# RWKV-7 recurrence: the last product of the triangular inverse in three 64x64 corners and two PSUM banks

## What is computed

```
def step(S, inp):                       # S: (value, key) state of each head
    rt, wt, kt, vt, at, bt = inp
    S = (S * wt[:, :, None, :] + jnp.einsum('bhvk,bhk->bhv', S, at)[..., None] * bt[:, :, None, :]
         + vt[..., None] * kt[:, :, None, :])
    return S, jnp.einsum('bhvk,bhk->bhv', S, rt)
S, ys = lax.scan(step, s0, xs)
```

## Time and profile before

| | |
|---|---|
| time, median of 3 runs | 3230.78 us (3226.53 to 3233.24) |
| the profiled execution | 3236.48 us, its span 3234.70 us |
| granted clock of PE, mean over the span | 0.969 |
| PE busy | 3023.7 us (93%), 32300 matmuls and as many weight loads |
| DVE / ACT / POOL busy | 1567.6 (48%) / 955.6 (30%) / 1332.6 us (41%) |
| the 16 items of the recurrence | about 1885 to 2350 us of the span |

### The profile page before, as it was taken

How to read it: one execution, slowest core, us unless ns; L and a number is a source line. 1 busy time by engine, 2 the same in 40 slices (tenths; PEclk the granted TensorE clock), 3 DMA queues, 4 the chain that set the end, 5 groups by cost and what they waited for, 6 DMA issues and landing times.

```text
span 3234.7 us, 73556 instructions
## 1 busy us (share of the span) xinstructions
PE 3023.7 (93%) x32300; PEld 2845.5 (88%) x32300; DVE 1567.6 (48%) x2107; ACT 955.6 (30%) x1640; POOL 1332.6 (41%) x1016
## 2 busy tenths in 40 slices
PE   7999988989999999989999889999878999999997
PEld 6989856889999999978999877777777999999996
DVE  5032254237666641244322156688624866663125
ACT  4132264233111121123311246666623211111112
POOL 3322310235777743341433323333232677774320
PEclk9999998999999999999999889999989999999998
DMA  3344453322223233112422313222142122324311
GB/s 101 119 135 111 144 169 110 97 79 79 79 79 112 79 131 143 52 45 103 170 92 92 100 46 98 65 61 72 47 169 91 60 79 80 114 81 134 139 42 61
DMA packets 342471, 312.25 MB, mean 97 GB/s; under 512 B 35335, under 2 KB 303059, under 8 KB 341020
## 3 DMA queue, kind: packets, MB, share of 16 engines
q1 hardware_dynamic: 325706, 275.99, 28.3%
q10 hardware_dynamic: 16466, 31.83, 2.6%
HBM read 212.79 MB, written 94.62 MB: 95 GB/s over the span
## 4 chain that ended last, share of the span: by engine, by line
PE 43%; DVE 4%; issue 3%; ACT 1%; SPq 1%; DMA 1%; POOL 1%; ACTq 0%; DVEq 0%; POOLq 0%
PE PS L521 17%; PE PS L688 12%; PE PS L2799 2%; PE PS L2811 1%; PE PS L2805 1%; PE PS L2793 1%; DVE act_lo L2516 1%; PE PS L2919 1%; PE PS L2789 1%; PE PS L702 1%; PE PS L2785 1%; PE PS L2844 0%; SPq L496 0%; PE PS L2950 0%; PE PS L2980 0%
## 5 line engine op out<-in xcount | busy, mean ns | idle before, releaser
L521 PE MATMUL PS<-act_hi,w_hi 128*128 128x344 f32 x1992 | 641.0, 322 | 38.3 <-DVE act_lo L2150 21.2
L521 PE MATMUL PS<-act_lo,w_hi 128*128 128x344 f32 x1992 | 637.8, 320 | 0.0
L521 PE MATMUL PS<-act_hi,w_lo 128*128 128x344 f32 x1992 | 637.3, 320 | 0.0
L502 POOL CAST w_hi<-w_raw 128x1024 fp32r<-128x1024 f32 (+1 forms) x119 | 129.1, 1085 | 1078.4 <-PE PS L521 561.2
L521 PEld LDWEIGHTS PS<-act_hi,w_hi 128*128 128x128 f32 x1992 | 376.4, 189 | 43.4 <-issue 28.3
L521 PEld LDWEIGHTS PS<-act_hi,w_lo 128*128 128x128 f32 x1992 | 376.4, 189 | 0.0
L521 PEld LDWEIGHTS PS<-act_lo,w_hi 128*128 128x128 f32 x1992 | 376.4, 189 | 0.0
L688 PE MATMUL PS<-T,wq_S 128*128 128x258 f32 x2880 | 365.7, 283 | 0.0
L688 PE MATMUL PS<-act_hi,wq_A 128*128 128x258 f32 x1920 | 364.5, 282 | 0.0
L688 PEld LDWEIGHTS PS<-T,wq_S 128*128 128x128 f32 x2880 | 354.4, 189 | 0.0
L688 PEld LDWEIGHTS PS<-act_hi,wq_A 128*128 128x128 f32 x1920 | 305.4, 190 | 0.0
(11 more groups left out here) (603 smaller groups left out, 5852.0 us busy)
## 6 DMA issues: line engine op xcount, KB each, us to landing
hidd<-hid_out SPq DMA_DIRECT2D x44, 516.0 KB, 3.3
w_raw<-in_ffn_w_gate_dram SPq DMA_DIRECT2D x44, 512.0 KB, 4.8
w_raw<-in_ffn_w_up_dram SPq DMA_DIRECT2D x44, 512.0 KB, 6.0
w_raw<-in_ffn_w_down_dram SPq DMA_DIRECT2D x32, 512.0 KB, 4.1
hid_in<-hidd SPq DMA_DIRECT2D x28, 516.0 KB, 7.2
proj<-stage ACTq DMA_DIRECT2D x24, 516.0 KB, 2.7
xT<-xkeep SPq DMA_DIRECT2D x3, 4128.0 KB, 16.6
rw<-z_st SPq DMA_DIRECT2D x24, 516.0 KB, 2.8
```

The lines of the kernel that those rows point to most:

```text
L502: nc.gpsimd.tensor_copy(w_hi[:, u, 0:kts, :], w_raw[:, u, 0:kts, :]).then_inc(w_hi_done, 1)
L521: mm = nc.tensor.matmul(PS[:, 3 * u + c, 0:CH], w[:, u, kt, :], x[:, kt, CH * c:CH * c + CH], start=(kt == 0 and part == 0), stop=(kt == k ...
```

## The change

pU is no longer 8 products of 128x128 weights with 64 columns, but for each head three products of 64x64 weights: the corners (0,0), (1,1) and (0,1) of the inverse; the fourth is zero. What has its rows in the lower half goes to bank 6 for rhs rows 0 to 63 and to bank 7 for rhs rows 64 to 127. So u's first 64 rows are PSUM bank 6, and its last 64 rows are the sum of bank 6 and bank 7. ACT copies both halves to q_u (a new step `u7` between `ysq` and `t8`), and DVE's step `u` becomes an addition on 64 partitions behind it. As bank 7 is now in use until u is made, the state's product K·V waits for `u` instead of `rhs`.

```diff
-        BA = Order(sem("sc_act"), "... rs:s ysq:o t8:i yln:o yrs:o ygn:o", AHEAD, -3, ITEMS + 1, ITEMS)
+        BA = Order(sem("sc_act"), "... rs:s ysq:o u7:n t8:i yln:o yrs:o ygn:o", AHEAD, -3, ITEMS + 1, ITEMS)
...
-                    for e in range(2):
-                        for q in range(GP):
-                            h = GP * e + q
-                            ins = mm(PS[:, 6, DH * h:DH * h + DH], i_XT[:, h, :], q_rhs[:, e, q, :], start=True, stop=True)
+                    for h in range(GH):
+                        rhs = [q_rhs[half(a), h // GP, h % GP, :] for a in range(2)]
+                        mm(part(h, 0, 0), i_XT[half(0), h, half(0)], rhs[0], start=(h == 0), stop=True, skip_group_check=True)
+                        mm(part(h, 1, 1), i_XT[half(1), h, half(1)], rhs[1], start=(h == 0), stop=True, skip_group_check=True)
+                        ins = mm(part(h, 0, 1), i_XT[half(0), h, half(1)], rhs[0], start=(h == 0), stop=True, skip_group_check=True)
                     ins.then_inc(BP.sem, BP.turn("pU", n))
...
                     pe.wait_ge(BA.sem, BA.of("tK", n))
-                    pe.wait_ge(BV.sem, BV.of("rhs", n))
+                    pe.wait_ge(BV.sem, BV.of("u", n))
...
+                if live_n:
+                    act.wait_ge(BP.sem, BP.of("pU", n))
+                    if n:
+                        act.wait_ge(BP.sem, BP.of("pY", n - 1))
+                        act.wait_ge(BP.sem, BP.of("pBU", n - 1))
+                    for a in range(2):
+                        ins = nc.scalar.copy(flat(q_u)[half(a), :], PS[half(a), 6 + a, :])
+                    ins.then_inc(BA.sem, BA.turn("u7", n))
...
-                    dve.wait_ge(BP.sem, BP.of("pU", n))
-                    nc.vector.tensor_copy(q_u[:, :, :, :].rearrange("p e q v -> p e (q v)"), PS[:, 6, :]).then_inc(BV.sem, BV.turn("u", n))
+                    dve.wait_ge(BA.sem, BA.of("u7", n))
+                    tt(flat(q_u)[half(1), :], PS[half(1), 6, :], flat(q_u)[half(1), :], ALU.add).then_inc(BV.sem, BV.turn("u", n))
```

More of the change, by code:

```diff
@@ L2595, in decoder_step @@
         BG = Order(sem("sc_pool"), "kp:s rk:s b:s rkm:i sum:o o:o R:s", AHEAD, -3, ITEMS + 1, ITEMS)
-        BA = Order(sem("sc_act"), "t16:n tV:i sq:s nc:i n:i xa:n t32:n xd:n w21:n tB:i x21:n t64:n t:s pe0:s rhs7:n iP:s tK:i t2:i y:o ln:s t4:i D:n rkc:i rs:s ysq:o t8:i yln:o yrs:o ygn:o", AHEAD, -3, ITEMS + 1, ITEMS)
+        BA = Order(sem("sc_act"), "t16:n tV:i sq:s nc:i n:i xa:n t32:n xd:n w21:n tB:i x21:n t64:n t:s pe0:s rhs7:n iP:s tK:i t2:i y:o ln:s t4:i D:n rkc:i rs:s ysq:o u7:n t8:i yln:o yrs:o ygn:o", AHEAD, -3, ITEMS + 1, ITEMS)
         BV = Order(sem("sc_dve"), "cs:s xs16:n x16:n mid:s st:o K:i ct:i S:o cc:s xi:i bv:i xt:i ak:i tr:n rhs:n rb:i xs2:i x2:i ss:s dm:n xs4:i x4:i kkn:s u:n xs8:i x8:i yn:o B:s A:s", AHEAD, -3, ITEMS + 1, ITEMS)
```

## The result

The changed kernel takes 3249.7 us (median of 4 runs, 3247.89 to 3251.89) against 3228.75 for the kernel before in the same comparison: 1.0069 times as long, 95% interval 1.0056 to 1.0082. That is 21 us more, where +4 was forecast and 3248 was the upper end of the range. The profiled execution took 3251.09 us, its span 3249.4 us; that is 14.7 us above the span of the profiled execution before, which itself lay above its median. So the two traces hold 14.7 of the 21 us.

A forecast was written before the change was run, and what follows sets the result against it. PE's work sets the pace, with code packets (7.1 per item, 3.94 us each) a second bound. 13 items by +0.5 us, less 2.5 at the ends, gave +4.0: about 3235 us, 8-in-10 range 3223 to 3248.

The forecast's parts named there:

- pU itself: In each item, pU's 48 passes of 64x64 weights take 0.94 us instead of 1.93 for 16 passes of 128x128.
- the rival of corners in series: pU's three corners run one after another, 3.2 us instead of 1.93: +20 us, 3251; chance 0.05.
- T8 starts 1.15 us after pU's start, x4 late next: Behind pU, T8 waits for DVE's x4, which pU doesn't move: 0.78 of the 0.99 us saved arrive.
- ACT and DVE: After pU, ACT's two copies take some 1.1 us, t8 starts 0.1 to 0.2 late, u slightly later; cost nothing.
- The mask: POOL's mask before y's first product doesn't depend on pU: of 0.78 us an item keeps 0.40 or 0.
- The code, in one item: With 64 more instructions, PE stops 1.3 to 1.5 us inside T8 for a packet; y's first product comes 0.66 us later.
- The code, over all items: Packet borders pass all positions, −0.4 to +0.9 us per item, mean +0.5: 13 items +6.5, less 2.5 at the ends.
- The ends: First item and last two, without the mask's limit or with PE slow, gain 0.8 us each: 2.5 us.
- code in full: Every item bound by code packets, 0.25 more of 3.94 us each: 1.0 us in 13 items, +10.5, 3241; chance 0.24.
- rival 4: Late u makes DVE's sample-update piece start behind POOL's mask, xs8 2.2 us late in six items: +13 us, 3244; chance 0.04.

The follow-up runs named there:

- u_path_piece_late: Changed kernel with the old pU product but u's new way, and piece 6 of the sample update moved to the end of DVE's pass: 3231.6 us, ratio 1.0004.
- after_cut64_piece_late: Changed kernel with half of T8 left out (1817 PE instructions per item again) and sample-update piece 6 at the end of DVE's pass: 3227.9 us, ratio 0.9994.
- after_piece_late: Changed kernel with piece 6 of the sample update moved from behind u to the end of DVE's pass: 3246.7 us, ratio 1.0044.
- u_path: Changed kernel with the old pU product of 128x128 weights, u still going the new way over ACT and DVE: 3243.7 us, ratio 1.0059.
- one_bank: Kernel before with pU as three corners all in bank 6, u made the old way, 65 more PE instructions per item: 3243.6 us, ratio 1.0059.
- after_shift128: Changed kernel with 128 more waits on a long-come semaphore in front of PE's recurrence, moving the code packets' borders: 3239.5 us, ratio 1.0037.
- plus64: Kernel before with the first half of T8's products issued twice, 64 more PE instructions per item: 3244.2 us, ratio 1.0037.
- plus64_x16: Kernel before with the first half of X16 issued twice, 64 more PE instructions per item: 3250.0 us, ratio 1.0064.
- after_cut64: Changed kernel with half of T8 left out, so 1817 PE instructions per item as in the kernel before: 3228.9 us, ratio 0.9995.

## Why the prediction was wrong, point by point

- **pU itself.** Right: 0.94 us was taken, and 0.94 is between the first and the last start. The corners with common rows run side by side, 0.01 us apart with 0.22 us each, so the rival of corners in series falls, and with it the rule of the Trainium skill, page "TensorE: Matmul & The Clock Gate", section "The mechanism", for this shape.
- **T8 starts 1.15 us after pU's start, x4 late next.** Right, 2247.05 less 2245.90.
- **ACT and DVE.** The two copies take 1.17 us (1.1 forecast), u starts 2.42 us after pU's start in the item at 2245.90 (2.2 forecast). Right that this costs nothing by itself: `u_path_piece_late`.
- **The mask.** Not contradicted: with less code and no lock a shorter pU brings nothing that can be measured (`after_cut64_piece_late`), but no run had a faster mask, so that it is the mask that takes the gain is not shown.
- **The code, in one item.** Right in kind: a stop of 1.3 to 1.5 us in T8 and the product 0.66 us late were worked out; 1.18 us and 0.57 us (6.75 less 6.18) are in the trace of the item at 2245.90. But the working was for the item with pU at 2123.31, and there the product came 2.13 us late (8.31 less 6.18): the packet's end fell into pU, another into X8, and the lock followed. That another item fits the working is luck.
- **The code, over all items.** This is the step that failed: "13 items by 0.5 = +6.5; less 2.5 us at the ends". From 1920.20 to 2303.62 before and from 1921.27 to 2320.08 after, the 13 items took 15.4 us more, 1.18 each and not 0.5; the last of them, at clock 1.00, took 2.5 more. A stop in T8 was counted, a second packet that ends in X8 or T16 of the same item was taken as short, and nothing was given to places outside the stretch. The time from pU's start to the product grew by 10.0 us over the 13 items, and the other 5.4 us came outside of it.
- **The ends.** The second part of that step. The prediction took 0.8 us off each of three passes for the shorter pU and gave them no code, although they grow by the same 64 instructions. Measured are 0.6 less, 1.2 more and 1.1 more, together 1.7 more instead of 2.5 less (and three times 0.8 are 2.4).
- **The clock.** It had no term. Of the 10.9 us in the ten items 6.3 are more busy time of PE, at a granted clock of 0.96 instead of 0.98; without them these ten would be some 0.45 us longer each (an estimate, 4.6 by ten), close to the +0.5 taken. The rival "code in full" has +1.0 per item, but for packets at 3.94 us alone; that 1.09 came out beside it is no proof of it.
- **The lock.** It was there as rival 4, with 0.04, and priced at 13 us; its margin of 0.6 us was figured from ACT's and DVE's own times only. What used the margin up is the other cost: a packet that ends inside pU delays u by 0.8 to 1.0 us (u starts 3.2 to 3.4 us after pU's start there, 2.42 elsewhere). It happens in three of the six items. What it costs the changed kernel is some 8 us by the medians of `after_piece_late`, with overlapping intervals. Two costs that were priced as separate cases were one chain.
- **Sum.** Of the 21 us the traces hold 14.7: 15.4 in the 13 items and 1.7 at the ends, less 2.4 outside the 16 passes. The other 6 us lie between one execution and the medians. The shares of the experiments don't add up (0.0059 for `u_path`, 0.0059 for `one_bank`, 0.0069 for both). One reason is in the traces: the corners shorten pU, so the piece falls behind the mask in three items instead of the six of `u_path`. Why taking 64 instructions away gives 24 us from the changed kernel but 8 from the kernel before is open; `after_shift128` says that the borders in the changed kernel may fall badly.

That PE stops at the ends of packets is shown by the traces; that more code costs time beyond its own work, by `plus64`, `plus64_x16` and `after_cut64`; that its place counts too, less firmly, by `after_shift128`. That the stops come from fetching is read from the packets' times and from the distances in multiples of 256 instructions; no run changed the fetch itself.

## What to carry to other kernels

Count instructions as well as time on an engine that runs long unrolled code in short steps: here 64 more PE instructions per item of 1817 cost 12 and 20 us of 3230 in two tests, some 5 us of it work, and the shorter pU could give PE at most 0.78 us per item, 12 us in all. Gaps that the profile calls "issue" and that lie multiples of 256 instructions apart are the sign, and a packet of instruction DMA some 2.5 us in front of them confirms it. Count the change in every item, those at the ends too, and compare the granted clock of the same stretch before the rest is explained. When two engines lock each other out, a margin has to be held against every delay that can come before it, those of the change's other half too.

## What the runs showed of the hardware that was not expected

- Code comes in packets of 256 instructions even in plain straight code, and PE stops at their ends for up to 1.8 us before the change and 2.4 us after it. The page "Runtime: NRT & Kernel Launch" of the Trainium skill, section "Instruction fetch mechanics", has the block size right and calls the fetch mostly hidden; here it was 23 to 42 us of stops in one recurrence.
- Corners (0,0) and (0,1) share their rows, and yet a round of all three passes takes 0.06 us, no more than a pass of one corner alone (1.07 us for 16).
- Moving the code of the changed kernel by 128 instructions, with waits that have long come, took 10 us off it (1.0069 to 1.0037); the same waits added 3 us to the kernel before, and 43 of them changed nothing.
- A DVE operation on two SBUF operands that starts while POOL's runs ends only 0.5 us after it: 2.32 us from 2127.44, when the mask ran until 2129.22, instead of 0.68. The same operation started before the mask, during the shorter operation ahead of it, took 1.37. The Trainium skill, page "SBUF — State Buffer", section "Terms", says that the loser of the port pair is blocked for the full instruction; the rows agree.
